# The end of a hybrid mixer layer on one core: silu, convolution products, value halves and output units in another order

## The chip, the cores and the metric

The kernel runs on one core of a Trainium2 chip. TensorE (PE) multiplies, VectorE (DVE), ScalarE (ACT) and GpSimd (POOL) do elementwise work, SyncE (SP) issues most transfers. The time is device microseconds of one execution; that of the kernel before is the median of three.

## The reference

A decoder trunk of two layers over 256 prompt positions and 8 sample sequences (264 columns together), all float32. A layer is a gated feed-forward block, a mixer, and a second such block, each with a norm before and after. The mixer, cut to what matters here:

```python
def conv_mixer(a, prev, dw, dw_bias, ln_g, ln_b, pw):
    g = a[..., :CONV_W] * jax.nn.sigmoid(a[..., CONV_W:])
    ...                                   # depthwise convolution of 31 taps -> y
    y = jax.nn.silu(layernorm(y, ln_g, ln_b)) @ pw

def pool_mixer(xb, prev, pos, pool_w, pool_scale):
    ...                                   # means over windows of 2, 4, 8, 16 minus x -> pooled
    y = jnp.einsum('btgc,gcd->btgd', pooled.reshape(B, T, POOL_GROUPS, POOL_GW), pool_w)
    y = y.reshape(B, T, POOL_W) * pool_scale

def sparse_attend(q, ks, vs, valid):
    s = jnp.einsum('btngd,btknd->btngk', qg, ks.astype(jnp.float32)) * HEAD_DIM ** -0.5
    p = jax.nn.softmax(jnp.where(valid[:, :, None, None, :], s, -jnp.inf), axis=-1)
    o = jnp.einsum('btngk,btknd->btngd', p, vs.astype(jnp.float32))

y = jnp.concatenate([y_c, y_p, y_a], axis=-1) @ w_out     # 1024 x 1024
```

Prompt positions attend to the 64 best of 256 keys, each sample sequence to the 256 best of 1024 cached keys and its own new one.

## The kernel before

All activations lie transposed, channels on the 128 partitions and the 264 positions along a row. Weights are streamed in **units** of 128 x 1024 floats through six buffers (`raw`). A unit is split into a high part (`w_hi`, ScalarE, line 379) and the rest (`w_lo`, VectorE, line 599) in three buffers (`SPLIT`), and each product of 128 x 128 x 264 is then three TensorE products (`three`, lines 1105 to 1107: hi x hi, hi x lo, lo x hi). A split waits for the unit three back to be done (`unit_done`). Units 9 to 15 of a mixer are used unsplit from `raw`. Unit 15 holds the pointwise weights of the convolution and of the pooling. Units 16 to 23 are `w_out`: eight **output units** of 24 products each. The mixture of their rows is: blocks 0 and 1 the convolution's outputs, 2 and 3 the pooling's, 4 to 7 the heads.

There is no scheduler. Each engine runs a program written out by hand, in that order, and waits on named counting semaphores.

The stretch in question is the end of `mixer`. There are four **prompt rounds** (`for j in range(4)` on ScalarE and TensorE): exponentials (line 509), transposes of the probabilities (1413), ScalarE's copy of them (527), products with the values (1429, 1430), then ScalarE's high part (533) and VectorE's low part (954) of the round's output into block 4 + j. Two rounds overlap. After them, before the change:

- VectorE takes the sample scores, their maximum (`s_smax`, 1023), the first pooling windows (978 to 986), the reciprocal of the sum (1027), scales all 1025 columns of `psm` (1028), makes `dg` (1030), the own key's probability of each head spread over columns, and does the other windows (991 to 998).
- ScalarE does the exponential of `psm` (535) between, then silu of the normalised convolution (539), in place in `cacc`.
- TensorE waits for `dg`, spreads it over the partitions with `ones` (1434), transposes `psm` in eight blocks (1436), waits for ScalarE's copy `pTs` (543), and does `values(0)` (1454): the first sequence of each of four pairs, 32 products into rows 32 q to 32 q + 7. Then the four products of the convolution (1465), the two of the pooling (1470), and `values(1)`, the second sequence of each pair.
- ScalarE and VectorE make high and low parts of both (547 and 1033, 550 and 1036); ScalarE copies the sample outputs to `osb` in four instructions (555); both split output unit 2 (`split(L, u0 + 18)`).
- TensorE does blocks 0 to 3 of output unit 0 (`half_out(0, True)`), two transposes of `osb` (1488), blocks 0 to 3 of unit 1, waits for the sample outputs' parts (VectorE 1042 to 1052, `o_slo`), and ends units 0 and 1. Units 2 to 7 follow whole.

On SyncE's queue the loads of output units 5 to 7 and of the next block stand behind a wait for `values(1)` (`v_used`), since the values lie in two of the six buffers; unit 5's buffer is that of unit 15, and is waited for too (`unit_done` of the pooling products). GpSimd's store of the pooling state waits for `values(1)`.

## Time and profile before

| | us |
|---|---|
| median of 3 | 1151.5 (1150.71 to 1151.86) |
| profiled execution | 1149.91 |
| its span, first to last instruction | 1148.3 |
| TensorE busy | 1082.8 (94% of the span) |
| VectorE, ScalarE, GpSimd busy | 741.7, 514.2, 190.1 |
| mean granted TensorE clock | 0.982 |

The span is read from the first to the last instruction; 1.6 us of the execution lie around it. A timeline row has the start, the time until the end of the last of its instructions, engine, line, operation, output and inputs, how many, and in brackets the idle time of the engine ahead of it and what ended it. Rows of TensorE overlap, since its ends are modelled. A float32 product is two records, a transpose or a split product one.

### The profile page before, as it was taken

How to read it: one execution, taken by the hardware profiler on the slowest of the kernel's cores; microseconds unless marked ns; L12 is line 12 of the kernel's file. 1: busy time of each engine (PE TensorE's matmuls, PEld its weight loads, DVE VectorE, ACT ScalarE, POOL GpSimd, SP SyncE). 2: the span in 40 equal slices, each digit the busy share in tenths (PEclk: the TensorE clock that was granted, in tenths of full speed). 3: DMA queues.
4: the chain of work that ended last, by engine and by line, in shares of the span. 5: the costliest groups of instructions: out<-in, count | busy, mean ns of one | idle time of the engine just before them, and what ended most of it. 6: DMA issues, size and time to landing. Idle time of an engine off the chain costs nothing.

```text
span 1148.3 us, 27626 instructions
## 1 busy us (share of the span) xinstructions
PE 1082.8 (94%) x9358; PEld 1025.1 (89%) x9358; DVE 741.7 (65%) x1211; ACT 514.2 (45%) x832; POOL 190.1 (17%) x241
## 2 busy tenths in 40 slices
PE   6999999999779999999999999999986799999996
PEld 6999999888448999999999999998863699999996
DVE  5676744788955766764476776448888466676544
ACT  5544433621444644443464444345215455444432
POOL 4211100411300311110041111004222022111001
PEclk9999999999879999999999999999998899999998
DMA  8464565343536355555435465563444445555541
GB/s 279 163 231 165 199 234 189 138 139 131 151 94 178 129 183 183 181 185 178 154 110 206 172 217 202 193 224 124 123 137 138 93 139 184 182 180 177 189 149 38
DMA packets 90465, 191.17 MB, mean 166 GB/s; under 512 B 12323, under 2 KB 48483, under 8 KB 90403
## 3 DMA queue, kind: packets, MB, share of 16 engines
q1 hardware_dynamic: 87426, 184.82, 48.7%
q0 software_dynamic: 2976, 5.53, 2.0%
q8 instruction: 38, 0.62, 0.2%
q14 instruction: 25, 0.20, 0.1%
HBM read 187.71 MB, written 2.59 MB: 166 GB/s over the span
## 4 chain that ended last, share of the span: by engine, by line
PE 85%; DVE 5%; ACT 3%; SPq 2%; issue 2%; DMA 1%; POOL 0%; DVEq 0%; POOLq 0%; ACTq 0%
PE PS L1105 23%; PE PS L1106 23%; PE PS L1107 23%; PE PS L1213 4%; SPq L263 2%; PE PS L1243 2%; PE PS L1141 2%; DVE w_lo L599 1%; PE PS L1153 1%; PE PS L1152 1%; PE PS L1156 1%; DVE rstd_post L628 1%; ACT w_hi L379 1%; PE PS L1454 1%; PE PS L1357 1%
## 5 line engine op out<-in xcount | busy, mean ns | idle before, releaser
L599 DVE TENSOR_TENSOR w_lo<-raw,w_hi 128x1024 fp32r<-128x1024 f32 x295 | 394.7, 1339 | 312.3 <-ACT w_hi L379 309.8
L379 ACT ACTIVATE w_hi<-raw 128x1024 fp32r<-128x1024 f32 x295 | 310.7, 1055 | 240.5 <-PE PS L1107 212.1
L1105 PE MATMUL PS<-x_hi,w_hi 128*128 128x264 f32 x1456 | 415.7, 286 | 0.7 <-DVE w_lo L599 0.6
L1106 PE MATMUL PS<-x_lo,w_hi 128*128 128x264 f32 x1456 | 412.5, 283 | 0.0
L1107 PE MATMUL PS<-x_hi,w_lo 128*128 128x264 f32 x1456 | 412.4, 283 | 0.0
L1105 PEld LDWEIGHTS PS<-x_hi,w_hi 128*128 128x128 f32 x1456 | 274.2, 188 | 2.3 <-DVE w_lo L599 1.6
L1106 PEld LDWEIGHTS PS<-x_lo,w_hi 128*128 128x128 f32 x1456 | 274.4, 188 | 0.1
L1107 PEld LDWEIGHTS PS<-x_hi,w_lo 128*128 128x128 f32 x1456 | 273.0, 187 | 0.0
L1105 PE MATMUL PS<-h_hi,w_hi 128*128 (+1 forms) x832 | 237.1, 285 | 3.4 <-issue 3.3
L1107 PE MATMUL PS<-h_hi,w_lo 128*128 (+1 forms) x832 | 236.9, 285 | 0.0
L1106 PE MATMUL PS<-h_lo,w_hi 128*128 (+1 forms) x832 | 236.2, 284 | 0.0
L1105 PEld LDWEIGHTS PS<-h_hi,w_hi 128*128 128x128 f32 x832 | 156.5, 188 | 4.3 <-issue 4.3
L1106 PEld LDWEIGHTS PS<-h_lo,w_hi 128*128 128x128 f32 x832 | 157.0, 189 | 0.0
L1107 PEld LDWEIGHTS PS<-h_hi,w_lo 128*128 128x128 f32 x832 | 156.6, 188 | 0.0
L1515 POOL TENSOR_TENSOR us<-gs,us 128x264 f32<-128x264 f32 x88 | 80.0, 909 | 431.9 <-DVE us L663 401.2
L426 ACT ACTIVATE gs<-gs 128x264 f32<-128x264 f32 x88 | 37.3, 424 | 194.3 <-DVE gs L657 194.3
L1528 POOL TENSOR_TENSOR h<-h,y 128x264 f32<-128x264 f32 x45 | 38.8, 893 | 327.9 <-DVE y L643 259.9
L1213 PE MATMUL PS<-x_all,raw 128*128 128x264 f32 x192 | 45.4, 389 | 0.0
L657 DVE TENSOR_TENSOR gs<-PS,rstd 128x264 f32<-128x264 f32 x88 | 37.9, 431 | 9.2 <-PE PS L1107 5.5
L1141 PE MATMUL PS<-sq,con 128*128 128x264 f32 x96 | 30.6, 401 | 11.3 <-DVE w_lo L1067 9.6
L1213 PEld LDWEIGHTS PS<-x_all,raw 128*128 128x128 f32 x192 | 35.7, 190 | 5.6
L671 DVE TENSOR_TENSOR h_lo<-us,h_hi 128x264 f32 x88 | 37.5, 426 | 0.0
(255 smaller groups left out, 1000.2 us busy)
## 6 DMA issues: line engine op xcount, KB each, us to landing
raw<-in_wts SPq DMA_DIRECT2D x312, 512.0 KB, 3.6
kv<-in_kT SPq DMA_DIRECT2D x128, 64.0 KB, 2.0
kx<-in_kxT SPq DMA_DIRECT2D x128, 32.0 KB, 2.1
vx<-in_vC POOLq DMA_DIRECT2D x48, 64.0 KB, 2.5
raw<-in_vC SPq DMA_DIRECT2D x32, 64.0 KB, 2.3
kv<-in_vC SPq DMA_DIRECT2D x32, 64.0 KB, 1.9
out_yT<-h SPq DMA_DIRECT2D x8, 132.0 KB, 1.8
vx<-in_vC SPq DMA_DIRECT2D x16, 64.0 KB, 1.9
```

The source lines that it names most:

```text
L379: act.activation(w_hi[:, u % SPLIT, :], raw[:, u % RAW, :], ACT.Copy) \
L426: act.activation(gs[:, f % 3, :], gs[:, f % 3, :], ACT.Silu).then_inc(sem["silu"], 1)
L599: tt(w_lo[:, u % SPLIT, :], raw[:, u % RAW, :], w_hi[:, u % SPLIT, :].bitcast(F32), AL.subtract) \
L657: tt(gs[:, f % 3, :], PS[:, 2 * (f % 3), 0:NT], rstd[:, :], AL.mult).then_inc(sem["gs"], 1)
L671: tt(out, us[:, f % 3, :], hi.bitcast(F32), AL.subtract).then_inc(sem["h_lo"], 1)
L1105: pe.matmul(out, w_hi[:, w, cols], hi, start=start, stop=False)
L1106: pe.matmul(out, w_hi[:, w, cols], lo, start=False, stop=False)
L1107: return pe.matmul(out, w_lo[:, w, cols], hi, start=False, stop=stop)
L1141: pe.matmul(PS[:, 7, 0:NT], ones, sq[:, ORDER[i], :], start=(i == 0), stop=(i == KD - 1)).then_inc(sem["mm_pre"], 1)
L1213: ins = pe.matmul(PS[:, m % 2, 0:NT], raw[:, (u0 + m) % RAW, col(k)], x_all[:, k, :], start=(k == 0), stop=(k == KD - 1))
L1515: pool.tensor_tensor(us[:, f % 3, :], gs[:, f % 3, :], us[:, f % 3, :], AL.mult).then_inc(sem["mid"], 1)
L1528: pool.tensor_tensor(h[:, d, :], h[:, d, :], y[:, d, :], AL.add).then_inc(sem["h_new"], 1)
```

## The change

The two layers run the same code, so each edit is made in both.

1. ScalarE does silu in round 2, between its copies of the probabilities and of the round's output, and loads the exponential's table (`warm(6, ACT.Exp)`) after round 3.
2. TensorE does the four convolution products right behind round 3, ahead of `dg`. They go to banks 6 and 7, `psm`'s blocks to banks 4 and 5.
3. VectorE does not scale `psm`. It scales the identity by the reciprocal (`spread`), and TensorE multiplies each block of `psm` by it in place of a transpose. `dg` gets the reciprocal as a second factor.
4. VectorE does the windows of 2 ahead of the wait for the exponential, all other pooling behind `dg` and the convolution's low part.
5. `values(0)` and `values(1)` stand in a row, both into bank 3, and ScalarE copies all 128 rows of them at once.
6. Output unit 2 is split earlier: on ScalarE with units 0 and 1, on VectorE between rounds. TensorE does blocks 0 and 1 of unit 0 ahead of the values, those of units 1 and 2 behind them, then the transposes of `osb`, the pooling products, blocks 2 and 3 of units 0 to 2, blocks 4 to 7 of units 0 to 2, and units 3 to 7 whole.

```diff
@@ ScalarE
-                for m in range(16, 18):
+                for m in range(16, 19):
                     split(L, u0 + m)
...
+                    if j == 2:
+                        act.wait_ge(sem["c_norm"], at_layer(L, "c_norm", 1))
+                        for c in range(2):
+                            ins = act.activation(cacc[:, c, :], cacc[:, c, :], ACT.Silu,
+                                                 scale=pars[:, LNG + c:LNG + c + 1],
+                                                 bias=pars[:, LNB + c:LNB + c + 1])
+                        ins.then_inc(sem["c_silu"], 1)
                     act.wait_ge(sem["o_p"], at_layer(L, "o_p", j + 1))
                     act.activation(h_hi[:, 4 + j, 0:NP], PS[:, 1, 0:NP], ACT.Copy).then_inc(sem["o_hi"], 1)
+                warm(6, ACT.Exp)
                 act.wait_ge(sem["s_smax"], at_layer(L, "s_smax", 1))
...
-                for q in range(4):
-                    ins = act.activation(osb[32 * q:32 * q + 8, :, :], PS[32 * q:32 * q + 8, 2:4, 0:128], ACT.Copy)
-                ins.then_inc(sem["o_sc"], 1)
-                split(L, u0 + 18)
+                act.activation(osb[:, :, :], PS[:, 3, 0:256].rearrange("p (a b) -> p a b", a=2), ACT.Copy) \
+                    .then_inc(sem["o_sc"], 1)
@@ VectorE
                 norm(3)
+                split(L, u0 + 18)
                 heads_out(2)
...
-                fours = windows_2_and_4()
+                twos = windows_2()
                 dve.wait_ge(sem["p_sexp"], at_layer(L, "p_sexp", 1))
                 after(L, step(L, dve.reciprocal(smx[:, 3:4], smx[:, 2:3])))
-                ts(psm[:, :], psm[:, :], smx[:, 3:4], None, AL.mult).then_inc(sem["p_snorm"], 1)
-                dve.wait_ge(sem["p_snorm"], at_layer(L, "p_snorm", 1))
-                ts(heads(dg[:, :]), own_rows, psm[:, PAST:], None, AL.mult).then_inc(sem["dg"], 1)
-                windows_8_and_16(fours)
+                ts(spread[:, :], ident, smx[:, 3:4], None, AL.mult)
+                ts(heads(dg[:, :]), own_rows, psm[:, PAST:], smx[:, 3:4], AL.mult, AL.mult).then_inc(sem["dg"], 1)
                 dve.wait_ge(sem["c_ohi"], at_layer(L, "c_ohi", 1))
-                tt(h_lo[:, 0:2, :], PS[:, 4:6, 0:NT], h_hi[:, 0:2, :].bitcast(F32), AL.subtract).then_inc(sem["c_olo"], 1)
+                tt(h_lo[:, 0:2, :], PS[:, 6:8, 0:NT], h_hi[:, 0:2, :].bitcast(F32), AL.subtract).then_inc(sem["c_olo"], 1)
+                windows_8_and_16(windows_4(twos))
@@ TensorE
                     ins.then_inc(sem["o_p"], 1)
+                raw_ready(pe, L, u0 + 15)
...
+                ins.then_inc(sem["c_out"], 1)
+
                 pe.wait_ge(sem["dg"], at_layer(L, "dg", 1))
                 pe.matmul(PS[:, 3, 256:320], ones, dg[:, :], start=True, stop=True)
                 for c in range(NPG):
-                    ins = pe.transpose(PS[:, 6 + c // 4, 128 * (c % 4):128 * (c % 4) + 128],
-                                       psm[:, 128 * c:128 * c + 128], ident)
+                    ins = pe.matmul(PS[:, 4 + c // 4, 128 * (c % 4):128 * (c % 4) + 128],
+                                    psm[:, 128 * c:128 * c + 128], spread[:, :], start=True, stop=True)
                 ins.then_inc(sem["p_st"], 1)
+                def out_part(o, ks):
+                    split_ready(L, u0 + N_IN + o)
+                    for k in ks:
+                        ins = three(PS[:, o, 0:NT], (u0 + N_IN + o) % SPLIT, col(k), h_hi[:, k, :], h_lo[:, k, :],
+                                    k == 0, k == KD - 1)
+                    return ins
+                pe.wait_ge(sem["c_olo"], at_layer(L, "c_olo", 1))
+                pe.wait_ge(sem["o_lo"], at_layer(L, "o_lo", 4))
+                out_part(0, (0, 1))
...
                 values(0)
...
                 values(1)
...
+                out_part(1, (0, 1))
+                out_part(2, (0, 1))
                 pe.wait_ge(sem["o_sc"], at_layer(L, "o_sc", 1))
                 for c in range(2):
                     ins = pe.transpose(PS[:, 7, 128 * c:128 * c + 128], osb[:, c, :], ident)
                 ins.then_inc(sem["o_st"], 1)
-                half_out(1, True)
-                pe.wait_ge(sem["o_lo"], at_layer(L, "o_lo", 4))
+                pe.wait_ge(sem["pool_y"], at_layer(L, "pool_y", 1))
+                for c in range(2):
+                    ins = pe.matmul(PS[:, 4 + c, 0:NT], raw[:, w, col(4 + c)], pw[:, c, :], start=True, stop=True)
+                ins.then_inc(sem["unit_done"], 1)
+
+                pe.wait_ge(sem["pl_olo"], at_layer(L, "pl_olo", 1))
+                for o in range(SPLIT):
+                    out_part(o, (2, 3))
                 pe.wait_ge(sem["o_slo"], at_layer(L, "o_slo", 1))
-                half_out(0, False).then_inc(sem["unit_done"], 1)
-                half_out(1, False).then_inc(sem["unit_done"], 1)
-                for o in range(2, KD):
+                for o in range(SPLIT):
+                    out_part(o, range(4, KD)).then_inc(sem["unit_done"], 1)
+                for o in range(SPLIT, KD):
```

On TensorE, from the last prompt round to the first value half, before:

```order
L1429 MATMUL PS<-pT,vn 64x256
L1430 MATMUL PS<-pT,vn 64x128
L1434 MATMUL PS<-dg,con 128x64
L1436 MATMUL PS<-con,psm 128x128 x8
L1454 MATMUL PS<-vx,pTs 8x128 x32
L1465 MATMUL PS<-cacc,raw 128x264 x4
L1470 MATMUL PS<-pw,raw 128x264 x2
```

The same place after; lines 1111 to 1113 are the three products of an output block, of which the first of two blocks is shown:

```order
L1435 MATMUL PS<-pT,vn 64x256
L1436 MATMUL PS<-pT,vn 64x128
L1444 MATMUL PS<-cacc,raw 128x264 x4
L1449 MATMUL PS<-dg,con 128x64
L1451 MATMUL PS<-spread,psm 128x128 x8
L1111 MATMUL PS<-h_hi,w_hi 128x264
L1112 MATMUL PS<-h_lo,w_hi 128x264
L1113 MATMUL PS<-h_hi,w_lo 128x264
```

The convolution's products have moved ahead of `dg`, the pooling's are gone from here, and a part of output unit 0 stands ahead of the values.

On VectorE, from the low part of round 3's output to the convolution's low part, before:

```order
L954 TENSOR_TENSOR h_lo<-PS,h_hi 128x256
L978 TENSOR_TENSOR pa<-pp 128x270
L979 TENSOR_TENSOR pb<-pp 128x270
L982 TENSOR_REDUCE pw<-stp 64x8 x4
L984 TENSOR_TENSOR pw<-pa 64x256
L986 TENSOR_TENSOR rtmp<-pb 128x268
L1027 RECIPROCAL smx<-smx 128x1
L1028 TENSOR_SCALAR psm<-psm,smx 128x1025
L1030 TENSOR_SCALAR dg<-con,psm 128x64
```

After:

```order
L956 TENSOR_TENSOR h_lo<-PS,h_hi 128x256
L980 TENSOR_TENSOR pa<-pp 128x270
L981 TENSOR_TENSOR pb<-pp 128x270
L1035 RECIPROCAL smx<-smx 128x1
L1036 TENSOR_SCALAR spread<-con,smx 128x128
L1037 TENSOR_SCALAR dg<-con,psm,smx 128x64
L1039 TENSOR_TENSOR h_lo<-PS,h_hi 128x528
L988 TENSOR_REDUCE pw<-stp 64x8 x4
```

The windows of 4 and more have moved from ahead of the reciprocal to behind the convolution's low part.

On ScalarE, in rounds 2 and 3, after (before, silu with its load stood behind the exponential of `psm`, and the second load was not there):

```order
L528 ACTIVATE pT<-PS 128x384 x2
L536 ACT_TABLE_LOAD
L536 ACTIVATE cacc<-cacc,pars 128x264 x2
L541 ACTIVATE h_hi<-PS 128x256
L528 ACTIVATE pT<-PS 128x384 x2
L541 ACTIVATE h_hi<-PS 128x256
L385 ACT_TABLE_LOAD
L385 ACTIVATE junk<-epsb 128x1
L544 ACTIVATE psm,smx<-psm,smx 128x1025
```

A second table load has come in, ahead of the exponential.

## Rows read from the trace of the kernel before

**Rows 1.** Page: busy time by engine, and the groups of the two splits.

```profile
PE 1082.8 (94%) x9358; PEld 1025.1 (89%) x9358; DVE 741.7 (65%) x1211; ACT 514.2 (45%) x832; POOL 190.1 (17%) x241
...
L599 DVE TENSOR_TENSOR w_lo<-raw,w_hi 128x1024 fp32r<-128x1024 f32 x295 | 394.7, 1339 | 312.3 <-ACT w_hi L379 309.8
L379 ACT ACTIVATE w_hi<-raw 128x1024 fp32r<-128x1024 f32 x295 | 310.7, 1055 | 240.5 <-PE PS L1107 212.1
```

**Rows 2.** Timeline of TensorE, layer 0, from round 3 to output units 0 and 1.

```profile
324.19 0.59 PE L1430 MATMUL PS<-pT,vn 128*64 128x128 f32 x3
330.27 0.69 PE L1434 MATMUL PS<-dg,con 128*128 128x64 f32 x2 [5.49 <-DVE dg L1030]
330.75 1.92 PE L1436 MATMUL PS<-con,psm 128*128 128x128 f32 x8
333.35 2.69 PE L1454 MATMUL PS<-vx,pTs 128*8 128x128 f32 x64 [0.69 <-ACT pTs L543]
335.97 2.05 PE L1465 MATMUL PS<-cacc,raw 128*128 128x264 f32 x8
337.86 1.05 PE L1470 MATMUL PS<-pw,raw 128*128 128x264 f32 x4
...
340.83 0.36 PE L1105 MATMUL PS<-h_hi,w_hi 128*128 128x264 f32 x1
...
345.97 0.36 PE L1105 MATMUL PS<-h_hi,w_hi 128*128 128x264 f32 x1 [1.63 <-issue]
```

**Rows 3.** Timeline of ScalarE, layer 0, same stretch; the last row follows unit 7.

```profile
322.53 0.39 ACT L533 ACTIVATE h_hi<-PS 128x256 fp32r<-128x256 f32 x1 [2.74 <-PE PS L1430]
...
326.47 1.15 ACT L535 ACTIVATE psm<-psm,smx 128x1025 f32<-128x1025 f32 x1 [1.27 <-DVE smx L1023]
...
327.73 1.28 ACT L539 ACT_TABLE_LOAD   x1
329.02 1.10 ACT L539 ACTIVATE cacc<-cacc,pars 128x264 f32<-128x264 f32 x2
332.70 0.60 ACT L543 ACTIVATE pTs<-PS 128x512 f32<-128x512 f32 x1 [2.58 <-PE PS L1436]
...
346.95 0.20 ACT L384 ACTIVATE junk<-epsb 128x1 f32<-128x1 f32 x1
...
366.62 0.39 ACT L408 ACTIVATE sq<-PS 128x264 f32<-128x264 f32 x1 [2.29 <-PE PS L1107]
```

**Rows 4.** Timeline of VectorE, layer 0, same stretch.

```profile
322.95 0.42 DVE L954 TENSOR_TENSOR h_lo<-PS,h_hi 128x256 fp32r<-128x256 f32 x1 [1.80 <-ACT h_hi L533]
...
328.96 0.16 DVE L1027 RECIPROCAL smx<-smx 128x1 f32<-128x1 f32 x1
...
329.94 0.27 DVE L1030 TENSOR_SCALAR dg<-con,psm 128x64 f32<-128x64 f32 x1
...
332.28 0.71 DVE L998 TENSOR_TENSOR pw<-pw,xp 128x528 f32<-128x528 f32 x1
```

**Rows 5.** Timeline of TensorE, layer 1: round 3 and the resumption.

```profile
889.27 0.59 PE L1430 MATMUL PS<-pT,vn 128*64 128x128 f32 x3
...
911.79 0.36 PE L1105 MATMUL PS<-h_hi,w_hi 128*128 128x264 f32 x1 [1.64 <-issue]
```

**Rows 6.** Chosen stretches: length, TensorE busy, granted clock, DMA share, GB/s.

```profile
895.00:901.50 6.50, 5.46 (x70) 0.50 0.01 3
...
344.30:345.90 1.60, 0.03 (x1) 1.00 0.89 317
...
881.10:883.20 2.10, 0.00 (x0) 1.00 0.41 116
883.30:884.40 1.10, 1.10 (x12) 1.00 0.46 130
884.60:887.80 3.20, 3.20 (x19) 0.50 0.44 127
```

**Rows 7.** Timeline of SyncE's queue: first loads behind the second value half.

```profile
340.83 4.56 SPq L256 DMA_DIRECT2D raw<-in_wts  x4
```

More of the change, by code:

```diff
@@ L213, in build @@
         nc01 = place("nc01", [128, 384], F32)
+        spread = place("spread", [128, 128], F32)
         assert s_kx[0] <= kx_end and s_gs[0] <= gs_end and s_sq[0] <= s_gs0
@@ L1050, in mixer @@
                 ins.then_inc(sem["o_ms"], 1)
+                dve.wait_ge(sem["pl_ohi"], at_layer(L, "pl_ohi", 1))
+                for c in range(2):
+                    ins = stt(h_lo[:, 2 + c, :], PS[:, 4 + c, 0:NT], pars[:, PSC + c:PSC + c + 1],
+                              h_hi[:, 2 + c, :].bitcast(F32), AL.mult, AL.subtract)
+                ins.then_inc(sem["pl_olo"], 1)
                 dve.wait_ge(sem["o_shi"], at_layer(L, "o_shi", 1))
@@ L1432, in mixer @@
                     ins.then_inc(sem["o_p"], 1)
+                raw_ready(pe, L, u0 + 15)
+                w = (u0 + 15) % RAW
+                pe.wait_ge(sem["c_silu"], at_layer(L, "c_silu", 1))
+                for c in range(2):
+                    for k in range(2):
+                        ins = pe.matmul(PS[:, 6 + c, 0:NT], raw[:, w, col(2 * k + c)], cacc[:, k, :],
+                                        start=(k == 0), stop=(k == 1))
+                ins.then_inc(sem["c_out"], 1)
                 pe.wait_ge(sem["dg"], at_layer(L, "dg", 1))
@@ L1458, in mixer @@
                 values(0)
-                raw_ready(pe, L, u0 + 15)
-                w = (u0 + 15) % RAW
-                pe.wait_ge(sem["c_silu"], at_layer(L, "c_silu", 1))
-                for c in range(2):
-                    for k in range(2):
-                        ins = pe.matmul(PS[:, 4 + c, 0:NT], raw[:, w, col(2 * k + c)], cacc[:, k, :],
-                                        start=(k == 0), stop=(k == 1))
-                ins.then_inc(sem["c_out"], 1)
-                pe.wait_ge(sem["pool_y"], at_layer(L, "pool_y", 1))
-                for c in range(2):
-                    ins = pe.matmul(PS[:, 6 + c, 0:NT], raw[:, w, col(4 + c)], pw[:, c, :], start=True, stop=True)
-                ins.then_inc(sem["unit_done"], 1)
-                values(1)
-                def half_out(o, first):
-                    split_ready(L, u0 + N_IN + o)
-                    for k in (range(4) if first else range(4, KD)):
-                        ins = three(PS[:, o, 0:NT], (u0 + N_IN + o) % SPLIT, col(k), h_hi[:, k, :], h_lo[:, k, :],
-                                    k == 0, k == KD - 1)
-                    return ins
-                pe.wait_ge(sem["c_olo"], at_layer(L, "c_olo", 1))
-                pe.wait_ge(sem["pl_olo"], at_layer(L, "pl_olo", 1))
-                half_out(0, True)
+                values(1)
+                out_part(1, (0, 1))
+                out_part(2, (0, 1))
                 pe.wait_ge(sem["o_sc"], at_layer(L, "o_sc", 1))
@@ L1489, in mixer @@
                 ins.then_inc(sem["o_st"], 1)
-                half_out(1, True)
-                pe.wait_ge(sem["o_lo"], at_layer(L, "o_lo", 4))
+                pe.wait_ge(sem["pool_y"], at_layer(L, "pool_y", 1))
+                for c in range(2):
+                    ins = pe.matmul(PS[:, 4 + c, 0:NT], raw[:, w, col(4 + c)], pw[:, c, :], start=True, stop=True)
[3 more added lines that the diff above has]
+                    out_part(o, (2, 3))
                 pe.wait_ge(sem["o_slo"], at_layer(L, "o_slo", 1))
-                half_out(0, False).then_inc(sem["unit_done"], 1)
-                half_out(1, False).then_inc(sem["unit_done"], 1)
-                for o in range(2, KD):
+                for o in range(SPLIT):
+                    out_part(o, range(4, KD)).then_inc(sem["unit_done"], 1)
+                for o in range(SPLIT, KD):
                     split_ready(L, u0 + N_IN + o)
```

29 lines of the change are left out of this document (10 added, 19 removed).

## The prediction

> **What bounds the kernel now.** I read the page first, then the chain of waits, then the timelines of the stretch that the edit touches, engine by engine, in both layers. TensorE is busy for 94% of the span [rows 1]: the kernel ends earlier only where TensorE stands still, or computes at its lower clock. So the reader should look for holes in TensorE's timeline between the last prompt round and the steady run of output units. In layer 0 the last round's products end at 324.78 us (324.19 + 0.59). Then TensorE waits 5.49 us for `dg`, which VectorE writes at the end of the sample softmax; it transposes the probabilities, waits 0.69 us for ScalarE's copy of them, does the first value half, the convolution's and the pooling's pointwise products, the second value half, and half of output units 0 and 1. There it waits 1.63 us more and resumes at 345.97 us; from then on it never stops until the last unit [rows 2]. That is 21.19 us, of which 7.8 us are waits. In layer 1 the same stretch takes 911.79 - 889.86 = 21.93 us [rows 3].
>
> The third cost is the clock. Behind the long wait the granted clock is 0.50 and stays there with TensorE at work: 6.5 us in layer 1 [rows 4]. It is 1.2 instead of 2.4 GHz, and all work of this stretch up to there takes twice as long.
>
> **Part by part, in layer 0, first with the clock held high.**
>
> *Silu between the rounds.* It needs a table load of 1.28 us and two passes of 1.10 us together, 2.38 us [rows 5]. ScalarE is idle for 2.74 us before its copy at 322.53 (longer in layer 1), and the normalised input is ready by then, so this is free, with 0.36 us to spare. Its price comes back as a load of the exponential's table after the last round: ScalarE is free at 326.47 - 1.27 = 325.20, the load ends at 326.48, the one-column instruction takes 0.20 more, and the exponential starts at 326.7, 0.2 us late [rows 5]. It then ends at 327.95 instead of 327.73. The Trainium skill ("ScalarE: Activation LUTs", What ACT_TABLE_LOAD costs) gives 2.66 us for a switch, since it adds a drain to the load. By that the exponential would start 1.4 us later still, and the gain would be 2.8 us smaller over both layers. The trace does not agree: the silu starts at 329.02, right behind the load that began at 327.73.
>
> *Convolution products ahead.* The four take 2.05 us [rows 2] and now stand in the hole that begins at 324.78, so they end at 326.83. They leave a wait of 1.9 us before `dg`.
>
> *Pooling behind the division, `spread` for the division.* Today VectorE does pooling windows until 328.96 though the exponential has ended at 327.73, and then needs 0.8 us more to scale all of `psm` [rows 6]. Now the reciprocal starts at 328.0, takes 0.19 with its gap, then `spread`, 128 columns, which no row shows: between the reciprocal's 0.16 and the 0.27 of `dg`; I take 0.2, and at most 0.07 hangs on it. Then `dg`, 0.27, and 0.06 until TensorE starts: 328.7 instead of 330.27. The convolution's low half now stands between: 0.71 us, as the last pooling instruction of the same width, until 329.4. All that VectorE did for pooling and softmax from the exponential's start at 326.47 to 332.99 is 6.5 us; even if all of that stood behind 329.4, pooling would be ready at 335.9, before TensorE asks at 337.2.
>
> *Transposes become products.* Eight transposes took 1.92 us at the low clock [rows 2]. A product in float32 costs (337.86 - 335.97) / 4 = 0.47 us for 264 columns at the high clock, so 0.23 for 128: eight take 1.83 us high, 3.66 us low. This is what the edit pays for dropping the 0.8 us on VectorE, and it makes it dependent on the clock.
>
> *The row of TensorE.* From 328.7: `dg` 0.24 (half of the 0.48 at the low clock), 1.83, 0.2 until the result is out, and 0.68 for ScalarE's copy and two hand-overs (332.67 to 333.35): 331.65. Six products of unit 0 hide that copy. Two value halves at 1.92 (338.91 to 340.83): 335.5. Twelve products of units 1 and 2 at 0.123, which is (366.6 - 345.97) / 168 [rows 2, 5]: 337.0. They hide the single copy of the values. Two transposes 0.25, pooling products 1.05: 338.2. Then the chain pooling products, ScalarE copy, VectorE low half is exposed: it takes 1.92, as from 338.91 to 340.83. Resume at 340.2, against 345.97, 5.8 us earlier. But before, 24 of the 192 output products were done at that point, and now 18; six more take 0.7. **Gain 5.1 us in layer 0, and 0.7 more in layer 1**, whose stretch is longer by that through the clock alone: 10.9 us.
>
> *What is moved and costs nothing.* The split of output unit 2 on VectorE (1.34 us by the page [rows 1]) goes into an idle time of 1.80 us [rows 6], on ScalarE into a long wait for the last chunk. On SyncE's queue the load of unit 5 and all behind it stand behind both the second value half and the pooling products; before, this was 340.83 [rows 7], now 338.2, so they come earlier. The pool states' store on GpSimd moves with the value half. The DVE split of unit 2 also no longer stands ahead of the sample outputs' sum, which removes the second old wait.
>
> *Then the clock.* Does a wait of 1.9 us keep it? Rows say both: after 1.60 us at 344.3, with dense work ahead, it stayed high; after 2.1 us at 881.1 it fell 1.2 us into the next work and stayed low for all of the 3.2 us row that follows [rows 4]. The change leaves two such waits a layer, four in all. A fall costs half of the row's 3.2 us, 1.6 us, where TensorE has work throughout. I take one fall in each layer: 3.2 us off. Forecast gain 10.9 - 3.2 = 7.7 us. The Trainium skill ("TensorE: Matmul & The Clock Gate", HAM oscillation) warns against long waits between bursts of products; by that rule these short ones would both keep the clock, and 10.9 us would come. The row of 881.1 speaks against relying on it.
>
> **The rivals.**
>
> *Clock high throughout* (10.9 us). For it: nothing is left near 5.49 us, and products replace transposes. Against: the row of 881.1. Time 1140.6 us.
>
> *Clock low as often as it can be.* Either all four waits cost 1.6 us: gain 4.5. Or it is low from `dg` on for 6.5 us as now: the probabilities then leave at 333.0, six low-clock products run until 334.3, the values end at 338.6, and TensorE resumes at 343.3: gain 1.9 and 2.7 us. Both give about 1146.9 us.
>
> *The split of unit 3 comes late.* All three split buffers are held by units begun ahead. Unit 0 closes 30 products after the resumption (3.7 us); the next split then needs 1.06 + 1.34 + 0.1 = 2.5 us [rows 1], ready at 6.2 us, and TensorE asks after 54 products, at 6.6. The margin is 0.4 us. If the splits take 1 us more it costs 0.6 us a layer, and if this repeats for unit 4, 2 to 3 us in all. With the low clock besides, the gain shrinks to about 2 us: 1149.5 us, no measurable change.
>
> *Slower:* the clock does not come back. The stretch now alternates short work and waits; if it stayed low from `dg` to the resumption, the probabilities take 3.66, values 6.9, twelve products 2.9, transposes 0.5, pooling 2.1, and the chain 1.92: resume at 348.6, 2.6 us late, with 0.7 for the six products 3.3 us in layer 0 and 2.6 in layer 1: 1157.4 us. At 6.5 us of low clock the gain is 1.9, and each further microsecond takes half of one, so it decides at about 10.3 us of low clock. The longest low stretch in these rows is 6.5 us.
>
> **How the numbers follow.** The profiled execution took 1149.91 us (span 1148.3), 1.6 below the median of 1151.5; the gain is taken from the median. One fall a layer: 0.42, 1143.8 us. High throughout: 0.27, 1140.6 us. Low as often as it can be: 0.21, 1146.9 us. Late splits and low clock: 0.06, 1149.5 us. Clock does not come back: 0.04, 1157.4 us. The range is 1139.8 to 1148.0 us: the high-clock case with 0.8 below it, and the low-clock one with 1.1 above it for what the two kernels' medians and the price of `spread` leave open. About 0.2% (2.3 us) is what a measurement of this kernel can tell from no change: faster by more 0.90, within 0.06, slower 0.04.
>
> **What the profile of the changed kernel would show.** `dg` on TensorE 3.9 us after the last round instead of 5.5, and the convolution products right at that round's end. The exponential 0.2 us after its old place, behind a table load. Eight products against `spread` in 1.8 us if the clock is high, 3.7 if low. No wait before the first value half. One wait of 1.9 us before the output units' third and fourth blocks, none later. Resume about 15.4 us after the last round, 2 to 3 more with a low clock. Wrong would be: ScalarE's copy of the third round later than TensorE's products by over 0.5 us (silu not hidden), waits for `w_lo` behind unit 2, or value products that wait for a transfer.

## The result and the profile after

| | before | after |
|---|---|---|
| median, us | 1151.11 (1148.54 to 1151.86, 4 runs) | 1138.88 (1137.74 to 1140.37, 4 runs) |
| ratio, 95% interval | | 0.9898, 0.9878 to 0.9919 |
| profiled execution, its span | 1149.91, 1148.3 | 1138.1, 1136.4 |
| mean granted TensorE clock | 0.982 | 0.988 |

The change is worth 12.2 us by the medians and 11.9 us by the spans. The forecast was 1143.8 us with a range from 1139.8 to 1148.0: the direction was right, the size too small, and the time lies 0.9 us below the range. It is nearest to the rival "clock high throughout" (1140.6 us).

A slip in the recorded prediction has to be named first: four of its group numbers are not those that stand over the printed rows. Its [rows 3] are the printed Rows 5 (TensorE, layer 1), its [rows 4] Rows 6 (the clock), its [rows 5] Rows 3 (ScalarE) and its [rows 6] Rows 4 (VectorE); 1, 2 and 7 agree. From here on the printed numbers are used.

The page of the kernel after, its engines, as [rows 1] before:

```profile
PE 1078.3 (95%) x9374; PEld 1024.2 (90%) x9374; DVE 740.0 (65%) x1211; ACT 513.5 (45%) x830; POOL 190.0 (17%) x241
```

TensorE's busy time fell by 4.5 us although 16 records were added: more of this stretch is computed at the higher clock. The rest of the gain, 7.4 of 11.9 us, is time in which it no longer stands still. Its timeline in layer 0, to be laid beside [rows 2]:

```profile
323.39 0.72 PE L1435 MATMUL PS<-pT,vn 128*64 128x256 f32 x3 [0.50 <-DVE h_lo L956]
...
323.98 0.57 PE L1436 MATMUL PS<-pT,vn 128*64 128x128 f32 x3
324.48 2.05 PE L1444 MATMUL PS<-cacc,raw 128*128 128x264 f32 x8
328.43 0.43 PE L1449 MATMUL PS<-dg,con 128*128 128x64 f32 x2 [1.91 <-DVE dg L1037]
328.70 2.00 PE L1451 MATMUL PS<-spread,psm 128*128 128x128 f32 x16
...
331.40 1.93 PE L1481 MATMUL PS<-vx,pTs 128*8 128x128 f32 x64
...
336.57 0.38 PE L1491 MATMUL PS<-con,osb 128*128 128x128 f32 x2
336.79 1.05 PE L1495 MATMUL PS<-pw,raw 128*128 128x264 f32 x4
339.71 0.39 PE L1111 MATMUL PS<-h_hi,w_hi 128*128 128x264 f32 x1 [1.87 <-DVE h_lo L1054]
```

The last round ends at 324.55 us (323.98 + 0.57) and TensorE resumes at 339.71, 15.16 us later; before it was 21.19 us. The 5.49 us wait is now 2.05 us of convolution products and a wait of 1.91. The waits of 0.69 and 1.63 are gone, and a wait of 1.87 for the pooling's low half is new. Layer 1, beside [rows 5]:

```profile
883.47 0.59 PE L1436 MATMUL PS<-pT,vn 128*64 128x128 f32 x3
...
887.95 0.43 PE L1449 MATMUL PS<-dg,con 128*128 128x64 f32 x2 [1.91 <-DVE dg L1037]
...
899.22 0.39 PE L1111 MATMUL PS<-h_hi,w_hi 128*128 128x264 f32 x1 [1.87 <-DVE h_lo L1054]
```

It is the same stretch again: 899.22 - 884.06 = 15.16 us, where it was 21.93. In both layers 18 output products are done at the resumption instead of 24; the six cost 0.73 us by the same products' steady rate. The stretches gain 21.19 - 15.16 - 0.73 = 5.3 us and 21.93 - 15.16 - 0.73 = 6.0 us, 11.3 of 11.9 us. The granted clock of chosen stretches (length, TensorE busy, clock, DMA share, GB/s) is what the forecast hung on:

```profile
326.60:328.40 1.80, 0.00 (x0) 1.00 0.53 141
328.50:331.00 2.50, 2.50 (x22) 1.00 0.48 134
337.90:339.60 1.70, 0.00 (x0) 1.00 0.61 75
339.80:343.80 4.00, 4.00 (x33) 1.00 0.43 55
```

Both waits, and the work behind both, have 1.00, where [rows 6] has 0.50 for 6.5 us. The same holds in layer 1.

It does not hold for every wait of this length. Ahead of the value products of round 1 TensorE also waits 1.85 us in this execution, and there the clock is 0.50 right behind the wait in layer 0, and from 1.5 us behind its end in layer 1:

```profile
314.34 1.05 PE L1435 MATMUL PS<-pT,vn 128*64 128x256 f32 x4 [1.85 <-DVE h_lo L956]
```

```profile
315.00:316.00 1.00, 1.00 (x7) 0.50 0.74 210
316.00:317.00 1.00, 1.00 (x6) 0.50 0.42 117
```

The kernel before has the same waits, of 1.85 and 1.86 us, with 0.50 behind both. What is said below of waits of 1.9 us is said of the two that the change leaves, ahead of `dg` and ahead of the third and fourth blocks.

ScalarE in layer 0, beside [rows 3]:

```profile
320.20 1.28 ACT L536 ACT_TABLE_LOAD   x1
321.50 1.10 ACT L536 ACTIVATE cacc<-cacc,pars 128x264 f32<-128x264 f32 x2
322.51 0.36 ACT L541 ACTIVATE h_hi<-PS 128x256 fp32r<-128x256 f32 x1
...
324.99 1.28 ACT L385 ACT_TABLE_LOAD   x1
326.28 0.20 ACT L385 ACTIVATE junk<-epsb 128x1 f32<-128x1 f32 x1
326.39 1.14 ACT L544 ACTIVATE psm<-psm,smx 128x1025 f32<-128x1025 f32 x1
```

And VectorE, beside [rows 4]:

```profile
321.46 1.22 DVE L601 TENSOR_TENSOR w_lo<-raw,w_hi 128x1024 fp32r<-128x1024 f32 x1
322.90 0.42 DVE L956 TENSOR_TENSOR h_lo<-PS,h_hi 128x256 fp32r<-128x256 f32 x1 [0.23 <-ACT h_hi L541]
...
327.65 0.16 DVE L1035 RECIPROCAL smx<-smx 128x1 f32<-128x1 f32 x1 [0.65 <-ACT psm L544]
327.85 0.29 DVE L1036 TENSOR_SCALAR spread<-con,smx 128x128 f32<-128x128 f32 x1
328.05 0.33 DVE L1037 TENSOR_SCALAR dg<-con,psm,smx 128x64 f32<-128x64 f32 x1
...
332.76 0.71 DVE L1004 TENSOR_TENSOR pw<-pw,xp 128x528 f32<-128x528 f32 x1
```

VectorE now waits for the exponential instead of arriving late with pooling windows, and the pooling is ready at 333.47, 3.3 us before TensorE asks.

### The profile page after: what moved, and what is told of

It is laid out like the page before. It is cut to its first block, busy times and chain, and to the rows that moved or that the text cites. A ratio compares the mean times of both kernels' runs of the same rounds, so it can differ in the third digit from the quotient of the medians.

```text
span 1136.4 us, 27658 instructions
## 1 busy us (share of the span) xinstructions
PE 1078.3 (95%) x9374; PEld 1024.2 (90%) x9374; DVE 740.0 (65%) x1211; ACT 513.5 (45%) x830; POOL 190.0 (17%) x241
## 4 chain that ended last, share of the span: by engine, by line
PE 85%; DVE 6%; ACT 4%; issue 2%; SPq 1%; DMA 1%; POOL 0%; DVEq 0%; POOLq 0%; ACTq 0%
PE PS L1111 24%; PE PS L1112 23%; PE PS L1113 23%; PE PS L1219 4%; PE PS L1147 2%; PE PS L1249 2%; DVE w_lo L601 1%; SPq L264 1%; PE PS L1158 1%; PE PS L1159 1%; PE PS L1162 1%; DVE rstd_post L630 1%; ACT w_hi L380 1%; PE PS L1225 1%; PE PS L1481 1%
## 5 line engine op out<-in xcount | busy, mean ns | idle before, releaser
L1111 PE MATMUL PS<-h_hi,w_hi 128*128 (+1 forms) x832 | 237.2, 285 | 3.7 <-DVE h_lo L1054 3.7
L1147 PE MATMUL PS<-sq,con 128*128 128x264 f32 x96 | 30.6, 402 | 11.9 <-ACT sq L579 10.2
```

The source lines that it names most:

```text
L1111: pe.matmul(out, w_hi[:, w, cols], hi, start=start, stop=False)
L1147: pe.matmul(PS[:, 7, 0:NT], ones, sq[:, ORDER[i], :], start=(i == 0), stop=(i == KD - 1)).then_inc(sem["mm_pre"], 1)
```

## The experiments

The theory after the result: the gain is time in which TensorE stood still or ran at 1.2 GHz in this stretch, and it is larger than forecast because the two waits of about 1.9 us that it leaves mostly do not cost the clock. The rivals: the clock had no part in it; the falls happen but are hidden; the gain comes from single parts such as `spread` or the third output unit begun ahead. All medians below are compared with the kernel before on the same chip: 1149.50 us for the first four kernels, 1150.21 for the next four, 1150.44 for the last two.

### The clock alone: work in the old wait

The kernel before, with ten products that nobody reads ahead of its wait for `dg`. The order is otherwise unchanged.

```diff
+                for _ in range(10):
+                    pe.matmul(PS[:, 0, NT:512], ones, con[:, C_COS:C_COS + 512 - NT], start=True, stop=True)
                 pe.wait_ge(sem["dg"], at_layer(L, "dg", 1))
```

> The kernel before, with ten products that nobody reads (ones by constants, 0.43 us each at the high clock) in TensorE's 5.49 us wait for dg. Nothing else is moved. Theory (the clock is a part of the cost of that wait): dg starts as before, but the transposes and the first value half run at the high clock; by the low stretches of the trace before this is worth 1.8 us in layer 0 and 2.6 us in layer 1, so about 4.4 us faster than before, near 1146.7 us. Rival (only the length of the waits counts, the clock's share is hidden or comes back later): within 1 us of before.

TensorE's timeline in layer 0:

```profile
327.76 4.45 PE L1434 MATMUL PS<-con 128*128 128x248 f32 x20
333.32 0.44 PE L1436 MATMUL PS<-dg,con 128*128 128x64 f32 x2 [1.11 <-DVE dg L1030]
333.59 1.05 PE L1438 MATMUL PS<-con,psm 128*128 128x128 f32 x8
335.32 1.93 PE L1456 MATMUL PS<-vx,pTs 128*8 128x128 f32 x64 [0.69 <-ACT pTs L543]
```

`dg` still comes 5.56 us after the start of the unread products (333.32 - 327.76), but the transposes take 1.05 us instead of 1.92 and the first value half 1.93 instead of 2.69 [rows 2], at a clock of 1.00. Median 1146.42 us, ratio 0.9968 (0.9955 to 0.998): 3.1 us, with no useful instruction added or moved. From `dg` to the resumption it is 1.8 us less than before in layer 0 and 2.6 less in layer 1, which is the 4.4 expected. But this profiled execution, at 1149.68 us the slowest of the six, is as long as that of the kernel before: the prompt rounds of layer 0, where the clock was 0.50 for 10 us on end, took 22.5 instead of 20.5 us, and another 2.3 us were lost ahead of the rounds of the two layers. So the 4.4 us are shown for the stretch, and some 3 us, by the medians, for the whole.

### The long wait alone

The kernel before, with silu ahead of ScalarE's copy of the third round, and the convolution's products ahead of the wait for `dg` (their results in two other banks). Nothing else.

```diff
 # ScalarE, round loop
+                    if j == 2:
+                        act.wait_ge(sem["c_norm"], at_layer(L, "c_norm", 1))
+                        for c in range(2):
+                            ins = act.activation(cacc[:, c, :], cacc[:, c, :], ACT.Silu, ...)
+                        ins.then_inc(sem["c_silu"], 1)
                     act.wait_ge(sem["o_p"], at_layer(L, "o_p", j + 1))
 # TensorE, behind the rounds; the same lines go behind values(0)
+                        ins = pe.matmul(PS[:, 6 + c, 0:NT], raw[:, w, col(2 * k + c)], cacc[:, k, :], ...)
                 pe.wait_ge(sem["dg"], at_layer(L, "dg", 1))
```

> The kernel before with two parts of the change: silu in round 2 (with the exponential's table load behind round 3) and the convolution's products ahead of dg. Transposes, the scaling of psm, the pooling's place, the value halves' places and the two half units stay as before. Theory: the products leave the path (1.83 us a layer), the exponential starts 0.2 us later but is hidden behind the pooling windows, and a wait of 3.6 us stays in which the clock still falls: 3.5 us faster than before, near 1147.5 us. Rival (the filled hole alone holds the clock): another 4 us, near 1143.5 us, with no granted clock of 0.50 behind dg.

TensorE's timeline in layer 0, and a stretch with its clock:

```profile
329.11 0.43 PE L1444 MATMUL PS<-dg,con 128*128 128x64 f32 x2 [3.30 <-DVE dg L1032]
...
331.17 3.00 PE L1464 MATMUL PS<-vx,pTs 128*8 128x128 f32 x60 [0.69 <-ACT pTs L545]
```

```profile
330.70:333.20 2.50, 2.03 (x40) 0.50 0.03 7
894.00:896.40 2.40, 2.19 (x44) 0.50 0.00 0
```

The wait is 3.30 us here (3.51 in layer 1), and the clock still falls, in both layers, though later and for a shorter time. Median 1145.72 us, ratio 0.9966 (0.9952 to 0.9979): 3.8 us, as expected (3.5). From `dg` to the resumption the profile has 13.3 us in both layers instead of 15.7 and 16.4. That is more than the 1.9 us of the products that left; the rest is less time at the low clock. Whether the gains of this kernel and of the one before it would add up was not tested.

### `spread` undone

The changed kernel with the eight transposes back in the place of the products, and with VectorE scaling `psm` again before `dg`.

```diff
-                    ins = pe.matmul(PS[:, 4 + c // 4, ...], psm[:, 128 * c:128 * c + 128], spread[:, :], start=True, stop=True)
+                    ins = pe.transpose(PS[:, 4 + c // 4, ...], psm[:, 128 * c:128 * c + 128], ident)
-                ts(spread[:, :], ident, smx[:, 3:4], None, AL.mult)
-                ts(heads(dg[:, :]), own_rows, psm[:, PAST:], smx[:, 3:4], AL.mult, AL.mult).then_inc(sem["dg"], 1)
+                ts(psm[:, :], psm[:, :], smx[:, 3:4], None, AL.mult).then_inc(sem["p_snorm"], 1)
+                dve.wait_ge(sem["p_snorm"], at_layer(L, "p_snorm", 1))
+                ts(heads(dg[:, :]), own_rows, psm[:, PAST:], None, AL.mult).then_inc(sem["dg"], 1)
```

> The changed kernel with VectorE scaling psm and TensorE transposing it, as before the change. Theory (spread trades VectorE time for TensorE time and is worth nothing at the high clock): dg starts about 0.5 us later, the eight transposes take about 1.1 us instead of 1.8, and the time is within 1 us of the changed kernel, near 1139 us. Rival (the removed 0.8 us on VectorE is a gain of its own): 1.6 us slower than the changed kernel, near 1140.5 us. A third: the longer wait ahead of dg lets the clock fall; then more than 2 us slower.

TensorE's timeline, layer 0, then layer 1:

```profile
329.95 0.43 PE L1450 MATMUL PS<-dg,con 128*128 128x64 f32 x2 [2.44 <-DVE dg L1038]
330.22 1.88 PE L1452 MATMUL PS<-con,psm 128*128 128x128 f32 x8
...
890.63 0.43 PE L1450 MATMUL PS<-dg,con 128*128 128x64 f32 x2 [2.44 <-DVE dg L1038]
890.90 1.05 PE L1452 MATMUL PS<-con,psm 128*128 128x128 f32 x8
```

The wait is 0.53 us longer, the transposes at the high clock 0.95 us shorter than the products. Median 1139.32 us, ratio 0.9904 (0.9887 to 0.9921), against 0.9898 for the change: no difference that these runs can tell. What `spread` saves on VectorE TensorE pays back, and a little more: in layer 1, where the clock held, `dg` comes 0.54 us later but the resumption 10.31 us after it instead of 11.27, so this stretch is 0.4 us shorter without `spread`. Against that stands the longer wait: the wait of 2.44 us cost the clock in layer 0 and not in layer 1 of the same execution.

### Pooling products ahead: the second wait taken away

The changed kernel with the pooling's products, and VectorE's low half of them, right behind the value halves, ahead of the twelve products that used to stand there.

```diff
 # TensorE
                 values(1)
+                pe.wait_ge(sem["pool_y"], at_layer(L, "pool_y", 1))
+                for c in range(2):
+                    ins = pe.matmul(PS[:, 4 + c, 0:NT], raw[:, w, col(4 + c)], pw[:, c, :], start=True, stop=True)
+                ins.then_inc(sem["unit_done"], 1)
                 out_part(1, (0, 1))
```

> The changed kernel with the pooling's products right behind the second value half and VectorE's low part of them ahead of the sample outputs' sum. Theory (the wait of 1.87 us is the chain product, copy, low part, and twelve products and two transposes can hide it): the wait falls to 0.2 us in each layer, 3.4 us faster than the changed kernel, near 1135.5 us. Rival (the sample outputs' chain is next and ends last): the wait only changes its name, to o_slo or to o_sc, and the gain is under 1 us.

TensorE's timeline in layer 0, then the clock of stretches in layers 0 and 1:

```profile
329.26 0.43 PE L1449 MATMUL PS<-dg,con 128*128 128x64 f32 x2 [1.91 <-DVE dg L1037]
329.53 3.54 PE L1451 MATMUL PS<-spread,psm 128*128 128x128 f32 x16
```

```profile
330.00:333.00 3.00, 3.00 (x16) 0.50 0.07 20
...
890.00:892.90 2.90, 2.90 (x15) 0.50 0.10 28
```

The second wait shrinks from 1.87 to 0.2 us. But the first, not touched and again 1.91 us, this time cost the clock in both layers: the eight products take 3.54 us instead of 2.00, so one fall costs 1.54 us. From `dg` to the resumption it is 11.19 us, against 11.28 with the second wait, which the fall ate up. The six executions of this one kernel run from 1135.49 us at a mean clock of 0.989 to 1140.81 at 0.982: the same instructions, 5.3 us apart, in the order of their clocks. The median, 1138.99 (0.99, 0.9881 to 0.9919), settles nothing on the second wait.

### The changed kernel, its two waits filled

Four unread products ahead of each wait.

```diff
+                for _ in range(4):
+                    pe.matmul(PS[:, 0, NT:512], ones, con[:, C_COS:C_COS + 512 - NT], start=True, stop=True)
                 pe.wait_ge(sem["dg"], at_layer(L, "dg", 1))
...
+                for _ in range(4):
+                    pe.matmul(PS[:, 6, NT:512], ones, con[:, C_COS:C_COS + 512 - NT], start=True, stop=True)
                 pe.wait_ge(sem["pl_olo"], at_layer(L, "pl_olo", 1))
```

> The changed kernel with four products that nobody reads in each of its two waits (1.7 us of 1.9), ahead of dg and ahead of the pooling's low part. Theory (the clock can still fall behind a wait of 1.9 us, as in the profile of pool_early, where it did in both layers, and did not in that of the changed kernel): the clock is 1.00 in all four places in the profile, the median is 0 to 3 us below that of the changed kernel (about 1137.5 us), and the fastest runs are no faster than the changed kernel's fastest. Rival (the clock is set by something else than the gap in work, or the changed kernel hardly ever loses it): the same median as the changed kernel, near 1139 us, and the same spread.

The waits that are left are 0.24 and 0.20 us, and the clock fell in neither layer. Median 1138.13 us, ratio 0.9892 (0.9876 to 0.9909), against 0.9898 (0.9878 to 0.9919) for the change: 0.7 us by the ratios, too small to be separated. That fits two waits that rarely cost anything. Had the change lost its clock twice in each execution, 3 us would have come back here, which lies at the edge of what the two intervals allow. The spread, 3.4 us, is no smaller than that of the change, 2.6, so these two waits are not what makes the executions differ: this profile, of the slowest of the four, is 2.6 us behind that of the change by what passes ahead of the rounds of the two layers.

### The pooling ahead and the first wait filled

```diff
 # the pooling ahead, as above, and
+                for _ in range(4):
+                    pe.matmul(PS[:, 0, NT:512], ones, con[:, C_COS:C_COS + 512 - NT], start=True, stop=True)
                 pe.wait_ge(sem["dg"], at_layer(L, "dg", 1))
```

> pool_early with four unread products in the wait ahead of dg. The second wait is 0.2 us there and needs none. Theory (in pool_early's profile 1.7 us a layer went out of the wait and came back as low clock): with both gone, dg to resumption takes 9.5 us in both layers instead of 11.2, and the median is 3 us below the changed kernel's, near 1136 us. Rival (pool_early's gain is lost elsewhere, on the chain behind it): dg to resumption is 9.5 us but the median stays near 1139 us.

From `dg` to the resumption it is 9.6 us in both layers, 1.7 less than in the changed kernel: the second wait is worth its own length once the clock holds. Yet the median is 1137.93 us (0.9893, 0.9877 to 0.9909), only 0.2 below the kernel with both waits filled. The windows of the mixer, from its prompt rounds to behind this stretch, say where a part of it went:

```profile
296.00:338.00 42.00, 32.23 (x338) 0.96 0.44 120
862.00:900.00 38.00, 30.45 (x295) 0.82 0.43 117
```

In layer 1 the clock is 0.82 on average, though the stretch itself is high throughout: it is low in the prompt rounds ahead of it, which take 22.4 us instead of 21.4 in the changed kernel's profile. That is 1.1 us. A larger part, 2.7 us, was lost between the resumption in layer 0 and the rounds of layer 1, where both kernels have the same instructions; the clock there was 0.50 from 846.8 to 853.4 us with TensorE at work throughout, and 1.00 in the changed kernel's profile from 838 to 862 us. Why it fell there stays open. The rounds led to the next kernel.

### Three waits of the rounds filled too

The kernel above, with four unread products ahead of the transposes of round 0, three ahead of the value products of round 1, and three ahead of the second half of the keys.

```diff
+                    if j == 0:
+                        for _ in range(4):
+                            pe.matmul(PS[:, 1, NT:512], ones, con[:, C_COS:C_COS + 512 - NT], start=True, stop=True)
                     pe.wait_ge(sem["p_norm"], at_layer(L, "p_norm", j + 1))
...
+                    if j == 1:
+                        pe.wait_ge(sem["c_rms"], at_layer(L, "c_rms", 1))
+                        for _ in range(3):
+                            pe.matmul(PS[:, 6, NT:512], ones, ..., start=True, stop=True)
                     if j:
                         pe.wait_ge(sem["o_lo"], at_layer(L, "o_lo", j))
...
                     if j == 2:
+                        for _ in range(3):
+                            pe.matmul(PS[:, 6, NT:512], ones, ..., start=True, stop=True)
                         keys(1)
```

> first_filled with unread products in three waits of the prompt rounds as well: four ahead of round 0's transposes (wait 2.37 us), three ahead of round 1's values (1.85), three ahead of the second key half (1.8 to 2.9). The second of them waits for ScalarE's square root first, long done. Theory (the rounds are set by VectorE and by the key transfers, TensorE's clock there hardly matters): within 1 us of first_filled. Rival (each low stretch of the rounds is on the path): the two low stretches a layer go, and 2 to 4 us with them, near 1133 us.

```profile
296.00:337.00 41.00, 34.62 (x356) 1.00 0.43 117
861.00:895.00 34.00, 28.12 (x307) 1.00 0.46 124
```

The corresponding windows have 1.00 in both layers. Median 1133.81 us (1133.70 to 1135.47), ratio 0.9863 (0.9847 to 0.988): 4.1 us below the kernel with the first wait filled, 16.4 below the kernel before. Of the two expectations on record, "within 1 us" is refuted and "2 to 4 us" came. That each low stretch of the rounds is on the path is not shown: between the two profiles the rounds of layer 1, which had 0.50 for 10 us of them, fall from 22.4 to 20.0 us, but those of layer 0, which had one low stretch of some 3 us, take 19.9 us in both. The other half of the 5.0 us between the two profiles lies ahead of the rounds, where the instructions are the same. These ten products a layer compute nothing; they only keep TensorE at work. This is the fastest kernel of the study.

### A longer first wait

The changed kernel with the pooling windows of 4 ahead of VectorE's wait for the exponential instead of behind the division.

```diff
-                twos = windows_2()
+                fours = windows_4(windows_2())
...
-                windows_8_and_16(windows_4(twos))
+                windows_8_and_16(fours)
```

> The changed kernel with the pooling's windows of 4 back ahead of the wait for the exponential. Theory (dg ends last on VectorE): the reciprocal starts 0.9 us later (1.6 us of windows, of which 0.65 fill VectorE's wait), the wait ahead of dg grows from 1.9 to 2.8 us, so 1.8 us slower than the changed kernel, near 1140.7 us, and up to 3 us more where that wait costs the clock. Rival (the pooling ends last, since the second value half leaves it little room): no slower.

VectorE's timeline in layer 0:

```profile
328.65 0.44 DVE L992 TENSOR_TENSOR rtmp<-pb 128x268 f32<-128x268 f32 x1
329.01 0.16 DVE L1035 RECIPROCAL smx<-smx 128x1 f32<-128x1 f32 x1
```

TensorE's clock behind the second wait, of 1.87 us, in layers 0 and 1:

```profile
343.70:346.50 2.80, 2.80 (x15) 0.50 0.59 72
...
907.00:909.80 2.80, 2.80 (x15) 0.50 0.88 80
```

The reciprocal no longer waits, and `dg` comes 1.06 us later in each layer. Median 1146.42 us (0.9973, 0.9959 to 0.9987), 7.5 us above the change (8.6 by the ratios to the kernel before on the same chip), where 1.8 to some 5 were expected: a miss. The span is 7.8 us longer. In it are 2 x 1.06 us of waiting, one fall behind the first wait (`dg` to the resumption is 12.84 us in layer 0, 11.27 in layer 1: 1.56 us), and one fall behind the second wait in each layer, some 1.6 us apiece (from the resumption in layer 1 to the end of the span it is 238.8 us instead of 237.2), together 6.8 us. The first part is the mechanism as the prediction described it; why the second wait, as long as ever, lost the clock here in both layers stays open.

### The changed kernel again

The kernel is unchanged; only the profile is taken anew.

> The changed kernel once more, unaltered, in five rounds. Theory (each wait of 1.9 us costs the clock in some executions and not in others, as in the profiles so far: lost in 4 of 10 such waits): the executions spread over 3 to 5 us, the slower ones with the lower mean clock, the median again near 1139 us. Rival (the changed kernel keeps the clock in these waits always): a spread of under 1.5 us and, in the profile, no clock of 0.50 behind dg or behind the pooling products.

TensorE's timeline in layer 0:

```profile
327.12 0.43 PE L1449 MATMUL PS<-dg,con 128*128 128x64 f32 x2 [1.91 <-DVE dg L1037]
...
338.41 0.39 PE L1111 MATMUL PS<-h_hi,w_hi 128*128 128x264 f32 x1 [1.87 <-DVE h_lo L1054]
```

Again no fall behind any of the four waits, and again 11.29 us from `dg` to the resumption. Median 1138.20 us (0.9898, 0.9881 to 0.9914), span 1135.5. The four executions lie 2.1 us apart, the slower two at the lower clock (0.988 against 0.990 and 0.991): less than the 3 to 5 us of the one expectation and more than the 1.5 of the other. With the four executions of the first measurement, 2.6 us apart, this kernel does lose the clock more in some executions than in others; whether it loses it in these two waits no trace shows.

### Two units begun ahead, not three

```diff
-                out_part(2, (0, 1))
...
-                for o in range(SPLIT):
+                for o in range(2):
                     out_part(o, (2, 3))
```

> The changed kernel with only output units 0 and 1 begun ahead; unit 2 is done whole behind them. Theory (twelve products hid a copy of 0.4 us, six do as well, and what is not done ahead is done behind): dg to resumption 0.7 us shorter, six products more behind it, the time within 1 us of the changed kernel, near 1139 us. Rival (the third unit fills a wait that comes back): up to 1.5 us slower.

`dg` to the resumption is 10.54 us instead of 11.28, with 12 products done instead of 18: the same rate, so nothing is lost and nothing gained there. The waits are still 1.91 and 1.87 us. Median 1139.48 us (0.991, 0.9893 to 0.9926), 1.3 above the changed kernel on the same chip, with intervals that overlap: no difference that these runs can tell. The profile's span is 1.7 us longer, but 1.8 us come in the rounds of the two layers and ahead of those of layer 0, which the edit does not touch.

## Why the prediction fell short, point by point

**The long wait and the order of the stretch: right, to a tenth.** Forecast: `dg` 3.9 us after the last round, the values 6.9 us after it, resumption 15.4. Measured: 3.88, 6.85 and 15.16 us. The two waits were forecast as 1.9 and 1.92 us and are 1.91 and 1.87. The products against `spread` take 2.00 us (1.83 forecast), the value halves (335.0 - 331.4) / 2 = 1.8 us each instead of 1.92, which is the 0.24 us by which the resumption came earlier than forecast. The stretches gain 11.3 us instead of 10.9.

**The step that failed: "I take one fall in each layer: 3.2 us off".** The price of a fall was right (1.54 us measured, 1.6 forecast). Its frequency was not: two of four waits were charged, and the profile of the changed kernel has none, nor has the second one. Over the profiles of the changed kernel and of its four variants that kept waits of 1.87 or 1.91 us, the clock fell behind 4 of 18 of them. By that rate the charge should have been 4 x 4/18 x 1.54 = 1.4 us. The falls came in two of the six profiles, twice in each, and in the other four not at all, so that the profile of the changed kernel has none is in part luck. The row of 881.1 in [rows 6], on which the step was built, was one wait. It was of 2.23 us (2.1 is the length of the window), and the clock had been 0.50 for the three microseconds right ahead of it; this study has longer waits that kept the clock (2.44 us, layer 1 of the kernel with transposes) and shorter ones that lost it. One row of the trace cannot carry the frequency of something that differs between executions. The Trainium skill's warning ("TensorE: Matmul & The Clock Gate", HAM oscillation), by which waits this short keep the clock, was nearer: it would have given 1140.6 us. The runs agree with it for 14 of the 18 waits and not for four, and they do not agree with it in the prompt rounds: there, in the ten profiles that have a wait of 1.85 or 1.86 us ahead of round 1's value products, the clock was 0.50 within 1.5 us of the end of all 19 such waits. Two of them stand in the trace of the kernel before, and neither the charge nor the rival weighed them. So the length of a wait does not settle it. What tells the waits of the rounds from the two that the change leaves, no run here shows.

**0.5 us from the rounds was not counted.** The last round of layer 0 ends 0.23 us earlier than before, and layer 1 is ahead by some 0.3 us more than its stretch explains. In layer 0 the second half of the keys' products ahead of round 3 runs at the high clock (1.92 us from 319.11; 3.41 before). In layer 1 the rounds, from their first transposes to their last value products, take 21.4 instead of 21.6 us; that was not traced to a row, and the change moved only silu and a split there. Over all profiles with unfilled rounds the same rounds take 19.9 to 22.5 us, so these 0.5 us may be no more than the luck of two executions. The last 0.3 us lie between the medians and the two profiled executions.

**The sum.** Forecast gain 7.7 us; 3.2 for the falls, 0.4 for the stretches, 0.5 for the rounds and 0.3 for the medians give 12.1 of the 12.2 us measured.

**Silu between the rounds: not quite free.** It was to have 0.36 us to spare. In layer 0 the keys' products before round 3 ran at the high clock, so ScalarE's idle time was shorter than in [rows 3], and its copy began at 322.51, 0.67 us after the products that it copies (321.44 + 0.40). This is over the 0.5 us that the prediction named as the sign of silu not being hidden. VectorE was at work on the split until 322.68, so silu costs 0.2 us of the 0.50 that TensorE waits; in layer 1, 0.79 us of idle time are left. In the total it is covered by the gain of the rounds. The table load went as forecast: 1.28 us, the silu right behind it, and the exponential starts 1.84 us after the last round (326.39 - 324.55) instead of 1.69 (326.47 - 324.78), 0.15 us late where 0.2 was forecast.

**Splits, loads and the slower rival: they did not come.** TensorE waited nowhere for `w_lo` behind unit 2, and SyncE's loads came behind the pooling products at 337.92 instead of 340.83. No low stretch of the changed kernel's end reached the 10.3 us from which the change would lose.

**The range.** 1139.8 to 1148.0 us left 0.8 us below the high-clock case, which had 0.27. With the frequency of falls unknown, and the value halves and rounds each able to give a few tenths, the low end should have been about 1138.5.

## What to carry to other kernels

Where TensorE alternates short work and waits, the clock is a cost of its own beside the waiting: here some 3 us of a 12 us gain, and 4 us more by the medians from ten unread products a layer in the rounds. Where the clock falls behind a wait only now and then, the wait should be priced by how often it did so at that place over several profiles, never by one row, and not by waits of the same length elsewhere. And look for low stretches well ahead of the place that is being edited: by the medians the largest gain left here lay in the rounds before it, not in the two waits that the change left. Last, single profiles differ by 2 to 3 us in places far from the edit; a gain should be read from the edited stretch in the profile and from the medians, not from the profile's span.

## What was not expected of the hardware

- Of the waits at the mixer's end, the same wait of 1.9 us keeps the clock in one execution and loses it in the next: 4 of 18 lost it, and 1 of 2 at 2.44 us. Waits of 2.97 and 2.98 us lost it in one layer of two, those of 3.30 us and more in all four cases, and filled ones (0.2 to 1.1 us left) never. In the prompt rounds of the same executions waits of 1.85 and 1.86 us lost it in 19 of 19 cases, and those of 2.37 us ahead of round 0's transposes were followed by 0.50 within 2 us in 17 of 22.
- At the high clock eight float32 transposes of 128 x 128 take 1.05 us and eight float32 products of the same shape 2.00.
- ScalarE's switch of tables cost 1.28 us each time in these rows, with the next instruction, where it had nothing else to wait for, 1.29 to 1.30 us after its start. The Trainium skill ("ScalarE: Activation LUTs", What ACT_TABLE_LOAD costs) adds a drain and comes to 2.66 us; no row here shows that drain.
